# Raw projection weights 12 to 26 issued by ScalarE behind its evictions, modulation loads left to SyncE

## What is computed

```python
shift, scale, gate = jnp.split(jax.nn.silu(c) @ w_mod + b_mod, 3, axis=-1)   # modulation, also for c_ctx
hc = rmsnorm(ctx, norm_g) * (1.0 + scale_c) + shift_c
hx = rmsnorm(x, norm_g) * (1.0 + scale_x) + shift_x
p = h @ w_in          # q, k, v, gates ..., for the tokens of x and, for k, v and the decays, of ctx
# gated linear attention over chunks, pooling branch, output projection, residual
# second block, with its own modulation silu(c_2) @ ada_w + ada_b, also for c_ctx_2:
# neighbourhood attention, spatial gating, convolution, gated feed-forward, final rmsnorm
```

## Time and profile before

| | |
|---|---|
| median of 3 runs | 2793.08 us (2792.84 to 2794.03) |
| the profiled execution, time | 2795.46 us |
| its span | 2793.7 us |
| TensorE matmuls busy | 2563.4 us, 92% of the span |
| VectorE, GpSimd, ScalarE busy | 53%, 38%, 26% |
| mean granted clock of TensorE | 0.958 of full speed |
| DMA, mean over the span | 116 GB/s |

### The profile page before, as it was taken

One profiled execution on the slowest core, in us unless ns is written; L12 is line 12 of the kernel. 1 busy time (PEld: TensorE's weight loads), 2 busy tenths in 40 slices (PEclk: granted clock), 3 DMA queues, 4 the chain that ended last, 5 costly groups with the idle time before them and its releaser, 6 DMA issues.

```text
span 2793.7 us, 33113 instructions
## 1 busy us (share of the span) xinstructions
PE 2563.4 (92%) x12016; PEld 2054.9 (74%) x12016; DVE 1490.1 (53%) x2191; ACT 727.0 (26%) x1208; POOL 1051.5 (38%) x493
## 2 busy tenths in 40 slices
PE   8889999999989779999895999979889999999997
PEld 4768787777768767777674778868667777777775
DVE  5793036574711256544888544466764444444446
ACT  4311243434300045212312354433221000011012
POOL 2233333333346433447651111113554444333344
PEclk9999999999999889999997799989999999999998
DMA  7674453434366753233311222251211111111111
GB/s 281 227 290 173 131 159 128 142 124 136 125 222 204 292 205 143 74 129 125 130 46 51 63 80 77 67 182 42 68 61 46 46 46 45 47 51 45 45 45 68
DMA packets 131232, 325.24 MB, mean 116 GB/s; under 512 B 11568, under 2 KB 59248, under 8 KB 125616
## 3 DMA queue, kind: packets, MB, share of 16 engines
q1 hardware_dynamic: 93392, 223.50, 24.1%
q10 hardware_dynamic: 37728, 100.22, 9.9%
HBM read 248.57 MB, written 70.39 MB: 114 GB/s over the span
## 4 chain that ended last, share of the span: by engine, by line
PE 49%; DVE 8%; issue 3%; ACT 1%; DMA 0%; DVEq 0%; POOL 0%; SPq 0%; ACTq 0%
PE pb L478 36%; PE g L2981 6%; PE g L3054 2%; PE pb L2981 1%; PE g L3034 1%; DVE zcs L2246 1%; PE g L2962 1%; DVE f_spare L2455 1%; PE g L2835 1%; DVE xl L2158 0%; DMA kept_in<-cs_d 0%; PE g L2960 0%; DVE hl L2525 0%; DVE ml L2462 0%; DVE cb L2504 0%
## 5 line engine op out<-in xcount | busy, mean ns | idle before, releaser
L845 POOL TENSOR_TENSOR w_hi<-w_raw,one 128x1024 fp32r<-128x1024 f32 x191 | 399.7, 2093 | 1543.1 <-PE pb L478 1136.1
L478 PE MATMUL pb<-xh,w_hi 128*128 128x512 f32 (+1 forms) x1224 | 485.9, 397 | 46.2 <-POOL w_lo L848 17.0
L848 POOL TENSOR_TENSOR w_lo<-w_raw,w_hi 128x1024 fp32r<-128x1024 f32 x191 | 510.1, 2671 | 15.0
L478 PE MATMUL pb<-xh,w_lo 128*128 128x512 f32 (+1 forms) x1224 | 477.1, 390 | 0.0
L478 PE MATMUL pb<-xl,w_hi 128*128 128x512 f32 (+1 forms) x1224 | 476.5, 389 | 0.0
L478 PEld LDWEIGHTS pb<-xh,w_hi 128*128 128x128 f32 x1224 | 235.7, 193 | 103.2 <-POOL w_lo L866 16.3
L478 PE MATMUL pb<-mh,w_hi 128*128 128x512 f32 x704 | 283.5, 403 | 15.0 <-DVE ml L2462 7.3
L478 PE MATMUL pb<-mh,w_lo 128*128 128x512 f32 x704 | 281.4, 400 | 0.0
L478 PE MATMUL pb<-ml,w_hi 128*128 128x512 f32 x704 | 281.2, 399 | 0.0
L478 PEld LDWEIGHTS pb<-xl,w_hi 128*128 128x128 f32 x1224 | 234.8, 192 | 51.6
L478 PEld LDWEIGHTS pb<-xh,w_lo 128*128 128x128 f32 x1224 | 235.4, 192 | 50.2 <-issue 1.0
(11 more groups left out here) (408 smaller groups left out, 4614.0 us busy)
## 6 DMA issues: line engine op xcount, KB each, us to landing
w_raw<-in_wall SPq DMA_DIRECT2D x205, 512.0 KB, 3.5
mod_later<-in_modw SPq DMA_DIRECT2D x28, 1024.0 KB, 6.1
proj_d<-stage ACTq DMA_DIRECT2D x40, 512.0 KB, 2.7
at_bias<-in_bias SPq DMA_DIRECT2D x64, 192.0 KB, 2.7
mod_raw<-in_modt SPq DMA_DIRECT2D x8, 1024.0 KB, 10.7
svt<-vt_d ACTq DMA_DIRECT2D x12, 512.0 KB, 4.6
vc<-proj_d SPq DMA_DIRECT2D x10, 512.0 KB, 5.7
vt_d<-spare_h ACTq DMA_DIRECT2D x10, 512.0 KB, 3.8
```

Of the source, the lines that this page charges most:

```text
L478: mm = pe.matmul(pb[bank][:, 0:n], w[:, b, wc:wc + P], x[:, k, tokens], start=(count == 0), stop=(count == total - 1))
L845: nc.gpsimd.tensor_tensor(w_hi[:, b, :], w_raw[:, b, :], one[:, 0:1].to_broadcast([P, 1024]), ALU.mult).then_inc(w_high, 1)
L848: nc.gpsimd.tensor_tensor(w_lo[:, b, :], w_raw[:, b, :], w_hi[:, b, :], ALU.subtract).then_inc(w_split, 1)
```

## The change

SyncE issues weights 2 and 3, then the first four modulation loads, then weights 4 to 11, and behind these a loop with modulation loads alone, 24 of them. Weights 12 to 26 are issued by ScalarE, weight t + 3 behind the store of tile t and, up to tile 13, the `w_hi` of tile t + 2. The waits of the loads are the same as before. ScalarE's two hardware loops over tiles are written out, since the loads stand among them.

```diff
--- before.py
+++ after.py
@@ -697,19 +697,15 @@
                     sp.wait_ge(p_vtr, p)
                 sp.dma_start(vc[:, :, :], rows_of(T_V, 8)[:, :, CHUNKS[p], :]).then_inc(p_in[b], 16)
 
-            weights(1, 5)
+            weights(1, 2)
             sp.wait_ge(gemv, 8)
             for p in range(4):
                 sp.dma_start(mod_later[:, p], modw[p]).then_inc(mod_in[p], 16)
+            weights(2, 6)
             with sp.Fori(0, 6) as i:
-                for b in range(2):
-                    sp.wait_ge(w_split, i * 2 + (b + 9))
-                    sp.dma_start(w_raw[:, b, :], wall2[i + 5, b]).then_inc(w_in[b], 16)
-                    for j in (2 * b, 2 * b + 1):
-                        sp.wait_ge(mod_free, i * 8 + (2 * j + 3))
-                        sp.dma_start(mod_later[:, j], modw4[i, j]).then_inc(mod_in[j], 16)
-            weights(11, 13)
-            weight(T_ZA + 1)
+                for j in range(4):
+                    sp.wait_ge(mod_free, i * 8 + (2 * j + 3))
+                    sp.dma_start(mod_later[:, j], modw4[i, j]).then_inc(mod_in[j], 16)
             sp.wait_ge(phase, 3)
             sp.wait_ge(tab_ready, 1)
             p_load(0)
@@ -1046,6 +1042,12 @@
                 act.wait_ge(t_ready, 2 * KT + k + 1)
                 act.activation(xh[:, k, T:TA], xin[:, k, T:TA], ACT.Identity,
                                bias=shift[:, 1, k:k + 1]).then_inc(xh_ready, 1)
+
+            def load_weight(t):
+
+                act.wait_ge(w_split, t - 1)
+                act.dma_start(w_raw[:, t % 2, :], wall[t]).then_inc(w_in[t % 2], 16)
+
             for t in range(HALVES, 2 * HALVES):
                 store_tile(t, proj_d[t], rows=stage_k, begin=H)
                 if t + 2 < 2 * HALVES:
@@ -1053,15 +1055,12 @@
                 if t == HALVES:
                     act.wait_ge(cond_in, 32)
                     act.activation(crow_sb[:, :, :], crow_sb[:, :, :], ACT.Silu).then_inc(cond_ready, 1)
-            kv_d = proj_d[2 * HALVES:T_LR].rearrange("(i j) p n -> i j p n", j=2)
-            q_d2 = proj_d[T_Q:T_ZA].rearrange("(i j) p n -> i j p n", j=2)
-            with act.Fori(0, (T_LR - 2 * HALVES) // 2) as i:
-                for b in range(2):
-                    store_tile(2 * HALVES + b, kv_d[i, b], i, 2, 6, rows=stage_k)
-            store_tile(T_LR, proj_d[T_LR], rows=stage_k)
-            with act.Fori(0, (T_ZA - T_Q) // 2) as i:
-                for b in range(2):
-                    store_tile(T_Q + b, q_d2[i, b], i, 2, 4, DK ** -0.5, rows=stage_k)
+                else:
+                    load_weight(t + 3)
+            for t in range(2 * HALVES, T_ZA):
+                store_tile(t, proj_d[t], scale=1.0 if t < T_Q else DK ** -0.5, rows=stage_k)
+                if t < T_ZA - 1:
+                    load_weight(t + 3)
 
 
             for b in range(2):
```

## The result

The changed kernel took 2763.19 us (median of four runs, 2758.92 to 2766.53) against 2793.56 us of the kernel before in the same comparison (2792.84 to 2797.59): ratio 0.9887, 95% interval 0.9874 to 0.9900. Compared once more, in five runs, it took 2763.50 us against 2788.98 us (nine runs, 2783.68 to 2795.11): 0.9911, interval 0.9895 to 0.9927. Applied to 2793.08 us, the first ratio is a gain of 31.6 us (27.9 to 35.2 by its interval) and the second one of 25 us (20.4 to 29.3); the forecast, 28.4 us, lies in both intervals.

What follows compares the result with a forecast made beforehand. Late weight loads behind SyncE's waits for VectorE stall TensorE in the first projection, which is otherwise TensorE-bound. -28.1 - 0.3 + 0 = -28.4 us takes 2793.08 to 2764.7 us, range 2762.5 to 2773.

Steps and rivals of the forecast that it cites:

- point 1: Weights 12 to 26 issued by ScalarE land in 6.0 us, within 9.7 us of cover: no TensorE stall.
- point 3: Weights 10 and 11 on SyncE ahead of VectorE waits: Silu 2 us sooner, 0.3 us of TensorE wait goes.
- point 4: ScalarE's 15 added weight issues, 0.36 us each, lie in idle time behind evictions and cost nothing.
- Point 2: First projection, tile 10 to tile 16's first unit: 28.1 us saved, 19.9 of stalls and 8.2 of lower clock.
- rival C: Weights land late (over 9.7 us), stalling tiles 12 to 15: 2780 to 2783 us, mildly 2768 to 2772; chance 0.07.
- Point 5: Four modulation loads moved up behind weight 3, at about 41 us: cost 0, at most a 4.0 us stall.
- Point 6: SyncE's modulation loop: VectorE goes on as before, ending near 239 us, hidden with about 41 us left.
- how the numbers follow: Range 2762.5 to 2773 us holds the forecast, B, the mild part of rival C, and 2 us between executions.
- A: Weight and modulation transfers fill the DMA engines and bound the stretch anyway: time stays near 2793 us; chance 0.03.
- B: Moved-up modulation loads delay weight 4: 1 to 4 us back, 2766 to 2769 us; chance 0.12.
- D: ScalarE is held in weight issues: 2769 us at 5.76 us each, 2799 at 10 us; chance 0.02 for a loss.
- E: VectorE becomes the bound of the phase, needing 41 us more: no gain; chance 0.01.

Runs made afterwards that it cites:

- tile-late experiment: Changed kernel with ScalarE issuing weight t+2 instead of t+3 behind the store of tile t, ahead of its `w_hi`: 2782.20 us.
- no context sums: Kernel before without the 16 sums for the context on VectorE, order and loads as before: 2774.18 us.
- merged order: Against the kernel before, all loads stay on SyncE but in an order merged by time, one to four modulation loads between later weights: 2761.25 us, ratio 0.9905.
- loads undone: Changed kernel with the first four modulation loads behind weight 9 again, weights 10 and 11 behind them: 2763.02 us, ratio 0.9910.

## Why the prediction was right in its sum and its range was too narrow

**What bounds the kernel** and points 1, 3 and 4: right. The stalls hung on SyncE's waits for `mod_free`, and what was won is what the hole had cost. Tiles 10 to 15 follow each other with nothing longer between them than the 0.2 us ahead of tile 13, ScalarE's issues cost nothing, and the eviction that held TensorE in the earlier trace rows holds it no more.

**Point 2**, the sum: 28.1 us forecast and 27.5 us measured, from eviction to eviction of tile 16's first unit (196.26 to 168.79). The difference is the first tile. Its first matmuls took 0.80 us instead of 0.60 us and ran at the lower clock for two matmuls longer, so TensorE was 0.95 us behind before it came to the hole. The second trace of the kernel before has the same delay, so it isn't of the change. Over all traces the phase ended at 309.1 and 310.1 before and at 281.5 and 280.7 after: 28.5 us between the means, with 28.4 forecast.

**Point 1's landing time** was too short, in a place where it did not show. I took 6.0 us from weights that shared SyncE's queue; on ScalarE's queue it was 7.3 us, and for weight 13 11.6 us, beyond the 9.7 us that I had given as the end of the cover. It was covered almost wholly, since the cover was longer than I had put it: ScalarE's issue leaves with `w_hi` and not behind it, 1.1 us into tile 11 (122.00, tile 11 at 120.86) and not 2.7, and `w_lo` took 2.75 us and not 3.08. The cover ended near 11.4 us, and tile 13 was held for the remaining 0.2 us. It was no single event: weight 13 took 11.0 us in the second trace of the changed kernel, and tile 13 was held as long there; in the run with the load ahead of `w_hi` it took 11.6 us again. My sign for C (over 9.7 us) went off, and ScalarE's waits for `w_raw`, forecast under 2 us, were 3.87 and 3.70 us. So rival C was nearer than its chance of 0.07 says; the tile-late experiment shows what it costs when the cover is gone.

**Point 5**: no cost, right. **Point 6**: hidden, right, but not "as before". VectorE ended its sums at 247.5 us and not at 239. It waited no more than before; its 56 sums of line 1729 took longer each. The group in the kernel before and in the changed one:

```profile
L1729 DVE CUSTOM_DVE_ANT_0 prod<-mod_later,crow_sb 128x1024 f32<-128x1024 f32 x56 | 81.5, 1456 | 13.4 <-ACT crow_sb L1055 9.0 <-DVE modx L1749 1.3 <-DMA mod_later<-in_modw 0.6
```

```profile
L1728 DVE CUSTOM_DVE_ANT_0 prod<-mod_later,crow_sb 128x1024 f32<-128x1024 f32 x56 | 89.1, 1592 | 11.5 <-ACT crow_sb L1057 7.1 <-DVE modx L1748 1.9
```

Of the 72 sums (with the context's) 11 took 2.8 to 3.5 us before and 15 after, the others 1.22 us. Each of the long ones had begun while a conversion of GpSimd (`w_hi` or `w_lo`) was under way, and ended 1.08 us behind that conversion's end; a sum of 1.22 us beside a conversion had begun ahead of it, and then the conversion ended late. One such pair, from the timelines of GpSimd and VectorE in the changed kernel:

```profile
235.95 3.27 POOL L844 TENSOR_TENSOR w_lo<-w_raw,w_hi 128x1024 fp32r<-128x1024 f32 x1
237.00 3.30 DVE L1728 CUSTOM_DVE_ANT_0 prod<-mod_later,crow_sb 128x1024 f32<-128x1024 f32 x1
```

With tiles coming faster 20 conversions fall beside the sums instead of 15. The cover of 41 us was 34.0 us.

**The step that failed** is the one that turned the sum into a range, in the part on how the numbers follow: "2 us for how single executions differ". I took it from three runs of the kernel before that agreed within 1.2 us. Over all its runs the kernel before took from 2783.68 to 2797.59 us, and the changed one 2758.92 to 2766.53; nine of the runs before, of one comparison on one chip, spread over 11.4 us, so it isn't only the chips that differ. The same part of the prediction says that 5.6 us is about what a measurement of this kernel can tell from no change, and yet gave the lower end 2.2 us. The part of the trace behind the phase varied by 5.5 us in two executions of one program. With such a scatter the ratio of a few runs is uncertain by several us: it gave 31.6 us in one comparison and 25 us in the next, on either side of 28.4. The range reached 2.2 us below the forecast and 8.3 us above it, since all my rivals but chance lay above; it should have reached some 5 us down. The mechanism isn't at fault: the phase became 28.5 us shorter where 28.4 us were forecast. What the prediction put at nothing is the 9.1 us behind the phase in the first pair of traces. The repeats show that one program differs by as much as 5.5 us there, and between the second traces of the two kernels only 2.4 us are left (2479.1 against 2476.8). How much of the 9.1 us is chance, and whether a lasting part is in them, stays open. That the result fell 1 us outside the range and not inside is luck of the draw: by the second ratio the time would be 2768.2 us, within it.

**Rivals.** A fell (no context sums, merged order), B fell (loads undone). C came as late weights, at a price of 0.2 us and not of whole stalls. D did not occur: ScalarE's issues took 0.35 to 0.58 us. E did not occur.

## What to carry to other kernels

In a hand-written list of waits and issues, each load goes at the pace of the slowest wait ahead of it. Look at the queue's own waits, and for any load that comes late compare the moment its own condition was met with the moment it was issued. Interleave by when the conditions come true, or use another engine's list; the second queue itself gained nothing here. Where the loads then go out on their own, look how near the latest of them comes to the moment it is wanted; here one was 0.2 us too late. And before a range is set, ask how far executions of the same program differ, by more than three runs and by a second trace.

## What the runs showed of the hardware

- One program's stalls are followed by the lower clock in one execution and not in the next: 0.48 us against 0.77 us for the same matmul. Ten traces had 174 to 216 us at the lower clock behind the phase, at 0.37 us of time for each of these.
- A 512 KB load landed in 4.2 us (median; longest 6.5) on SyncE's queue in the merged order, and in 7.3 us (longest 11.6; 7.2 and 12.9 in the second trace) on ScalarE's queue beside 1 MB loads on SyncE's; the last three on ScalarE's queue, behind all of these loads, took 4.1 to 4.5 us. The Trainium skill, DMA: Bandwidth & Descriptors, section Queues, rings and completion order, says that each DMA engine takes turns between the queues that have work, packet by packet. The long landings beside SyncE's loads fit with that; no run here separates it from the different moments of issue.
- A DMA issue of ScalarE started 0.03 us after the activation ahead of it had started, 1.03 us before that ended.
- VectorE's sums (128 x 1024) and GpSimd's conversions took turns: 1.22 us for a sum by itself, and for each that began during a conversion an end 1.08 us behind that conversion's, up to 3.47 us in all (15 of 72 in the changed kernel).
